# Gate and up bias of the experts: from TensorE products to rows loaded per job, spread by POOL and added by VectorE

## What is computed

```python
logits = jnp.dot(hf, w_router) + b_router
top_v, top_e = lax.top_k(logits, TOP_K)
top_w = jax.nn.softmax(top_v, axis=-1)
...
gu = xb @ w_gate_up[e] + b_gate_up[e]
gate = jnp.minimum(gu[:, 0::2], SWIGLU_LIMIT)
up = jnp.clip(gu[:, 1::2], -SWIGLU_LIMIT, SWIGLU_LIMIT)
act = (up + 1.0) * gate * jax.nn.sigmoid(SWIGLU_ALPHA * gate)
return act @ w_down[e] + b_down[e]
```

## Time and profile before

| | us |
|---|---|
| median of three runs | 1778.43 |
| lowest, highest | 1777.51, 1779.88 |
| profiled execution | 1780.92 |
| its span, first to last instruction | 1779.2 |
| mean granted TensorE clock, share of full | 0.977 |
| TensorE busy, share of the span | 1691.0, 95% |

### The profile page before, as it was taken

One profiled execution on the slowest core, in us unless ns is written; L12 is line 12 of the kernel. 1 busy time (PEld: TensorE's weight loads), 2 busy tenths in 40 slices (PEclk: granted clock), 3 DMA queues, 4 the chain that ended last, 5 costly groups with the idle time before them and its releaser, 6 DMA issues.

```text
span 1779.2 us, 43354 instructions
## 1 busy us (share of the span) xinstructions
PE 1691.0 (95%) x18644; PEld 885.3 (50%) x18644; DVE 577.8 (32%) x1366; ACT 350.2 (20%) x809; POOL 164.9 (9%) x250
## 2 busy tenths in 40 slices
PE   5999897689999888999999999999999999999997
PEld 2444896367478883434434434434434434434433
DVE  3679444664134564112112112112112112112211
ACT  3142321455222331101101101101101101101101
POOL 4000610101000001000000000000000000100100
PEclk9999999789999998999999999999999999999998
DMA  9950000401131259999999999999999999999991
GB/s 339 354 190 1 3 4 3 172 1 49 47 142 48 96 208 338 371 398 395 384 393 395 389 390 394 383 392 395 386 390 396 380 395 402 384 388 398 390 381 43
DMA packets 98345, 489.61 MB, mean 275 GB/s; under 512 B 15131, under 2 KB 17240, under 8 KB 48997
## 3 DMA queue, kind: packets, MB, share of 16 engines
q1 hardware_dynamic: 88326, 471.06, 67.4%
q0 software_dynamic: 7504, 16.80, 4.1%
q10 hardware_dynamic: 2448, 0.78, 0.2%
HBM read 478.87 MB, written 19.28 MB: 280 GB/s over the span
## 4 chain that ended last, share of the span: by engine, by line
PE 61%; DVE 0%; issue 0%; ACT 0%; POOLq 0%; DVEq 0%
PE bank L2090 37%; PE bank L2101 18%; PE bank L2075 1%; PE bank L2114 1%; PE bank L2081 1%; PE bank L2102 1%; PE bank L2091 1%; PE bank L2124 0%; DVE sb_y L2290 0%; POOLq L1979 0%; ACT sb_xT L2183 0%; DVE sb_mod L2281 0%; DVE sb_xT L2264 0%; ACT sb_wT L2206 0%; DVE sb_mod L2275 0%
## 5 line engine op out<-in xcount | busy, mean ns | idle before, releaser
L2090 PE MATMUL bank<-sb_w_raw,sb_xT 128*32 128x512 f32 x4608 | 668.7, 594 | 2.5 <-ACT sb_xT L2183 1.4
L2091 PE MATMUL bank<-sb_w_raw,sb_xT 128*32 128x512 f32 x1536 | 668.2, 594 | 0.0
L2090 PEld LDWEIGHTS bank<-sb_w_raw,sb_xT 128*32 128x32 f32 x4608 | 186.4, 110 | 455.9 <-issue 452.8
L2101 PE MATMUL bank<-sb_w_raw,sb_aT 128*32 128x256 f32 x4608 | 339.6, 381 | 2.0 <-DVE sb_aT L2271 2.0
L2102 PE MATMUL bank<-sb_w_raw,sb_aT 128*32 128x256 f32 x1536 | 339.2, 381 | 0.0
L2101 PEld LDWEIGHTS bank<-sb_w_raw,sb_aT 128*32 128x32 f32 x4608 | 188.5, 110 | 131.7 <-DVE sb_y L2290 2.3
L2275 DVE TENSOR_SCALAR sb_mod<-bank 128x256 f32<-128x256 f32 x96 | 40.5, 422 | 626.9 <-ACT sb_mod L2194 626.9
L2102 PEld LDWEIGHTS bank<-sb_w_raw,sb_aT 128*32 128x32 f32 x1536 | 166.9, 110 | 0.0
L2091 PEld LDWEIGHTS bank<-sb_w_raw,sb_xT 128*32 128x32 f32 x1536 | 166.3, 110 | 0.0
L2194 ACT ACTIVATE sb_mod<-bank 128x256 f32<-128x256 f32 x96 | 29.9, 384 | 655.6 <-PE bank L2091 655.6
L2290 DVE SCALAR_TENSOR_TENSOR sb_y<-bank,sb_prob_now,sb_mod 96x256 f32<-96x256 f32 x96 | 40.4, 474 | 215.1 <-PE bank L2102 215.1
(11 more groups left out here) (454 smaller groups left out, 1997.2 us busy)
## 6 DMA issues: line engine op xcount, KB each, us to landing
sb_w_raw<-in_w_gate_up_dram SPq DMA_DIRECT2D x256, 1024.0 KB, 8.1
sb_w_raw<-in_w_down_dram SPq DMA_DIRECT2D x128, 1024.0 KB, 8.5
sb_ring<-in_w_in_dram SPq DMA_DIRECT2D x7, 2048.0 KB, 10.0
sb_x<-in_ada_w_dram SPq DMA_DIRECT2D x8, 1024.0 KB, 9.0
sb_mod<-in_ada_w_dram SPq DMA_DIRECT2D x8, 1024.0 KB, 9.2
sb_ring<-in_ada_w_dram SPq DMA_DIRECT2D x3, 2048.0 KB, 14.0
sb_x<-in_x_dram SPq DMA_DIRECT2D x2, 2048.0 KB, 12.6
sb_ring<-in_w_out_dram SPq DMA_DIRECT2D x2, 2048.0 KB, 7.7
```

The costliest lines, as they stand in the source:

```text
L2090: te.matmul(up_bank[r][at, :], g.xT[:, k, at], g.w_raw[:, s, 512 * r:512 * r + 512], start=False, stop=last)
L2091: mm = te.matmul(up_bank[r][CAP:P, :], g.xT[:, k, STRIP * r:STRIP * r + STRIP], g.w_raw[:, s, 512 * G:2048], start=False, stop=last)
L2101: te.matmul(down_bank[j][at, 0:256], g.aT[:, k, at], g.w_raw[:, s, 1024 * r + 256 * j:1024 * r + 256 * j + 256], start=first, stop=last)
```

## The change

The bias rows are written once to DRAM with the one added to their odd entries. For every job ScalarE's queue loads the 8 KB row into one partition, POOL spreads it over all partitions (`partition_broadcast`, 1536 elements into `g.bias` and 512 into `g.last_quarter`), ScalarE copies the last quarter into partitions 96 to 127 of `g.bias`, and VectorE adds `g.bias` to the three banks into a new SBUF tile `g.biased`, from which gates and clips now read. The weights' products start the accumulation themselves. In the routing phase the bias takes two loads, two small ScalarE operations and two writes; the low parts are gone. At the start of the expert phase TensorE runs 20 filler products in place of the bias products.

```diff
+def load_bias(g, eng, e):
+    eng.dma_start(g.bias_row[0:1, :], g.bias_rows[e, :]).then_inc(g.row_in, 16)
...
 phase_route, sync
-            for i in range(2):
-                sp.dma_start(g.bias_raw[N_EXP * i:N_EXP * i + N_EXP, :, :], ...).then_inc(bias_in, 16)
-                at = slice(64 + N_EXP * i, 64 + N_EXP * i + N_EXP)
-                for j in range(G):
-                    sp.dma_start(g.bias_raw[at, j, :], g.a["b_gate_up"][0][:, 512 * G:]).then_inc(bias_in, 16)
+            sp.dma_start(wide_bias, g.a["b_gate_up"][0][:, 0:512 * G]).then_inc(bias_in, 16)
+            sp.dma_start(narrow_bias, g.a["b_gate_up"][0][:, 512 * G:]).then_inc(bias_in, 16)
...
+            sp.wait_ge(*act.at("bias_up"))
+            sp.dma_start(g.bias_rows[:, 0:512 * G], wide_bias).then_inc(g.bias_out, 16)
+            sp.dma_start(g.bias_rows[:, 512 * G:], narrow_bias).then_inc(g.bias_out, 16)
             for k in ks[4:]:
                 load_up(g, sp, k, slice(0, 1), k)
 phase_route, gpsimd: three memsets of g.pick go
 phase_route, scalar
-            sc.wait_ge(bias_in, 16 * (2 + 2 * G))
-            sc.copy(pairs(g.bias)[:, :, 0], pairs(g.bias_raw)[:, :, 0]).then_inc(*act("bias_even"))
-            sc.activation(pairs(g.bias)[:, :, 1], pairs(g.bias_raw)[:, :, 1], ACT.Identity, bias=g.ones[:, 0:1]).then_inc(*act("bias_hi"))
+            sc.wait_ge(bias_in, 16 * 2)
+            for part in (wide_bias, narrow_bias):
+                up = part.rearrange("p (n a) -> p n a", a=2)[:, :, 1]
+                mm = sc.activation(up, up, ACT.Identity, bias=g.ones[0:N_EXP, 0:1])
+            mm.then_inc(*act("bias_up"))
...
+            sc.wait_ge(g.bias_out, 16 * 2)
+            load_bias(g, sc, slice(0, 1))
 phase_route, vector
-            ve.wait_ge(*act.at("bias_hi"))
-            for i in range(2):
-                at = slice(64 * i + N_EXP, 64 * i + 2 * N_EXP)
-                raw, hi = pairs(g.bias_raw)[at], pairs(g.bias)[at]
-                ve.tensor_tensor(hi[:, :, 0], raw[:, :, 0], hi[:, :, 0].bitcast(F32), ALU.subtract)...
-                ve.scalar_tensor_tensor(hi[:, :, 1], raw[:, :, 1], 1.0, hi[:, :, 1].bitcast(F32), ALU.add, ALU.subtract)...
 phase_experts, sync
             e = expert(sp, last)
+            sp.wait_ge(g.row_in, 16 * last + 32)
 phase_experts, tensor
-            def bias_rows():
-                for b in range(G):
-                    mm = te.matmul(up_bank[b][:, :], g.bias_pick[:, :], g.bias[:, b, :], start=True, stop=False)
-                return mm
...
-                last = k == UP - 1
+                first, last = k == 0, k == UP - 1
...
-                        te.matmul(up_bank[r][at, :], ..., start=False, stop=last)
+                        te.matmul(up_bank[r][at, :], ..., start=first, stop=last)
...
-            te.wait_ge(*first_vec.at("bp0"))
-            bias_rows().then_inc(*first_pe("bias"))
+            for _ in range(20):
+                te.matmul(down_bank[2][:, 0:P], g.ones[:, :], g.ones[:, :], start=True, stop=True)
             te.wait_ge(x_in, 16)
...
                 activations_turned(turn, pe)
-                te.wait_ge(*vec.before("bp", turn))
-                bias_rows().then_inc(*pe("bias"))
 phase_experts, scalar
+            def quarter():
+                return sc.copy(g.bias[CAP:P, :, :], g.last_quarter[CAP:P, :].unsqueeze(1).broadcast_to([STRIP, G, 512]))
             def gated(b):
-                gate = up_bank[b][:, :].rearrange("p (n a) -> p n a", a=2)[:, :, 0]
+                gate = g.biased[:, b, :].rearrange("p (n a) -> p n a", a=2)[:, :, 0]
...
-            sc.wait_ge(used[UP - 1], 1)
+            sc.wait_ge(*pool.credit())
+            quarter().then_inc(*first_act("quarter"))
+            load_bias(g, sc, bass.ds(sc.value_load(g.table[0:1, 2:3], min_val=0, max_val=N_EXP - 1), 1))
             for b in range(G):
+                sc.wait_ge(*first_vec.at(f"ad{b}"))
                 gated(b).then_inc(*first_act(f"gc{b}"))
...
                 turned_copy().then_inc(*act("aT"))
-                sc.wait_ge(*done(UP_DONE, turn))
+                sc.wait_ge(*pool.at("spread", turn))
+                sc.wait_ge(*vec.before("ad2", turn))
+                quarter().then_inc(*act("quarter"))
+                load_bias(g, sc, bass.ds(expert(sc, turn + 2), 1))
                 sc.wait_ge(*vec.before("ac2", turn))
                 for b in range(G):
+                    sc.wait_ge(*vec.at(f"ad{b}", turn))
                     gated(b).then_inc(*act(f"gc{b}"))
 phase_experts, gpsimd
+            def spread():
+                po.partition_broadcast(g.bias[:, :, :].rearrange("p b n -> p (b n)"), g.bias_row[0:1, 0:512 * G])
+                return po.partition_broadcast(g.last_quarter[:, :], g.bias_row[0:1, 512 * G:])
             last = last_job(po)
+            po.wait_ge(g.row_in, 16)
+            spread().then_inc(*pool.credit())
...
             with po.Fori(0, last) as turn:
+                po.wait_ge(g.row_in, 16 * turn + 32)
+                po.wait_ge(*vec.before("ad2", turn))
+                po.wait_ge(*act.before("quarter", turn))
+                po.wait_ge(ticked, 3 * turn + 1)
+                tick(2)
+                spread().then_inc(*pool("spread"))
                 po.wait_ge(*vec.at("row", turn))
-                po.wait_ge(ticked, 2 * turn + 1)
+                po.wait_ge(ticked, 3 * turn + 2)
                 tick(0)
                 gather_rows(g, po, g.row[0:CAP, 0:1])
 phase_experts, vector (bias_pick and its uses go)
+            def added(b):
+                return ve.tensor_tensor(g.biased[:, b, :], up_bank[b][:, :], g.bias[:, b, :], ALU.add)
             def clipped(b):
-                ups = up_bank[b][:, :].rearrange("p (n a) -> p n a", a=2)[:, :, 1]
+                ups = g.biased[:, b, :].rearrange("p (n a) -> p n a", a=2)[:, :, 1]
...
+            ve.wait_ge(*first_act.at("quarter"))
+            ve.wait_ge(used[UP - 1], 1)
+            for b in range(G):
+                added(b).then_inc(*first_vec(f"ad{b}"))
...
                 turned_copy().then_inc(*vec("aT"))
-                ve.wait_ge(*pe.at("bias", turn))
-                bias_pick(bass.ds(turn + 2, 1)).then_inc(*vec("bp"))
+                ve.wait_ge(*act.at("quarter", turn))
+                ve.wait_ge(*done(UP_DONE, turn))
+                for b in range(G):
+                    added(b).then_inc(*vec(f"ad{b}"))
```

More of the change, by code:

```diff
@@ L1691, in phase_route @@
         merge = rows[:, 128:160]
+        wide_bias = g.bias[0:N_EXP, :, :].rearrange("p s n -> p (s n)")
+        narrow_bias = g.bias[N_EXP:2 * N_EXP, 0, :]
         mask, block_sum, mask_one = g.mask, g.block_sum, rows[:, 256:384].rearrange("p (t e) -> p t e", t=NT)
@@ L1987, in phase_experts @@
         up_bank, down_bank, turn_bank = ps[0:3], ps[3:6], ps[6:8]
-        pe = Turns(g.sem(ctx, "m_pe"), ["tr0", "tr1", "bias", "xt0", "xt1"])
-        act = Turns(g.sem(ctx, "m_act"), ["aT", "gc0", "gc1", "gc2", "xh", "y"])
-        vec = Turns(g.sem(ctx, "m_vec"), ["aT", "bp", "uc0", "ac0", "uc1", "ac1", "uc2", "ac2", "row", "xl", "share", "goal", "yw", "y"])
+        pe = Turns(g.sem(ctx, "m_pe"), ["tr0", "tr1", "xt0", "xt1"])
+        act = Turns(g.sem(ctx, "m_act"), ["aT", "quarter", "gc0", "gc1", "gc2", "xh", "y"])
+        vec = Turns(g.sem(ctx, "m_vec"), ["aT", "ad0", "ad1", "ad2", "uc0", "ac0", "uc1", "ac1", "uc2", "ac2", "row", "xl", "share", "goal", "yw", "y"])
+        pool = Turns(g.sem(ctx, "m_pool"), ["spread"])
         used = [g.sem(ctx, f"used{i}") for i in range(SLOTS)]
@@ L1997, in phase_experts @@
         x_in, y_out = g.x_in, g.sem(ctx, "y_out")
-        first_pe = g.steps(ctx, "first_pe", ["bias", "xt0", "xt1", "wT"] + names("bd{}", 3) + ["xt2"])
-        first_act = g.steps(ctx, "first_act", ["xh", "wT", "gc0", "gc1", "gc2"])
-        first_vec = g.steps(ctx, "first_vec", ["bp0", "y", "xl", "bp1"] + [x for i in range(2 * NT) for x in (f"gb{i}", f"xb{i}")] + [x for b in range(G) for x in (f"uc{b}", f"ac{b}")])
+        first_pe = g.steps(ctx, "first_pe", ["xt0", "xt1", "wT"] + names("bd{}", 3) + ["xt2"])
+        first_act = g.steps(ctx, "first_act", ["xh", "wT", "quarter", "gc0", "gc1", "gc2"])
+        first_vec = g.steps(ctx, "first_vec", ["y", "xl"] + [x for i in range(2 * NT) for x in (f"gb{i}", f"xb{i}")] + names("ad{}", G) + [x for b in range(G) for x in (f"uc{b}", f"ac{b}")])
         last_pe = g.steps(ctx, "last_pe", ["tr0", "tr1", "d"])
@@ L2008, in phase_experts, with expert @@
         UP_DONE, DOWN_DONE = SPARE - 1, UP - 1
+        def expert(eng, job):
+            return eng.value_load(g.table[0:1, bass.ds(job + 1, 1)], min_val=0, max_val=N_EXP - 1)
         def last_job(eng):
@@ L2036, in _ @@
         def _(sp):
-            def expert(job):
-                return sp.value_load(g.table[0:1, bass.ds(job + 1, 1)], min_val=0, max_val=N_EXP - 1)
             def rest_of_turn(turn, e, after):
@@ L2056, in _ @@
             with sp.Fori(1, last) as turn:
```

(12 more changed lines are left out.)

35 lines of the change are left out of this document (12 added, 23 removed).

## The result

The changed kernel takes 1760.76 us (median of four runs, 1758.08 to 1767.13) against 1779.16 us for the kernel before on the same chip: a ratio of 0.9911, 95% interval 0.9891 to 0.993. The forecast was 1762.2 us. The profiled execution took 1759.59 us (span 1757.8) against 1780.92.

What follows compares the result with a forecast made beforehand. TensorE was taken to set the 33.55 us turn, DMA close behind with some 22 us of loads in hand. Terms -21.7 + 2.2 + 1.6 + 1.7 = -16.2 us gave 1762.2 us; range 1753 to 1771, 8 in 10.

Steps and rivals of the forecast that it cites:

- The matmuls out of the loop, -21.7 us: Head of each loop turn: three bias matmuls leave TensorE's path, 0.70 us in each of 31 turns, at most -26.0.
- Additions under cover: VectorE in the loop: three additions, 2.06 us ahead of the clips, cost nothing since 6 us remain before TensorE's transposes.
- Spread on POOL "1.9 us, nothing": POOL's two broadcasts in each turn: 1.9 us taken from a memset's rate, 20.8 at the dear end, covered either way.
- 22 in hand: Cover for POOL's spread in a loop turn: TensorE waits at its transposes only once the spread takes over 22 us.
- Rival (b): TensorE's transposes in the loop: POOL's spread outlasts its cover, 9.3 us wait a turn, 2050 us total; chance 0.05.
- The row's own DMAs: nothing: Bias row load in each turn: 8 KB on ScalarE's queue against 12 MB on SP's costs nothing.
- DMA at the shorter turn: nothing, at most 1 us: Weight loads at 32.85 us turns: even needing 33.55 us they bind only at the very end, under 1 us.
- Rival (a): Loop: DMA becomes the bound, needing say 34.0 us a turn, total 1776.6 us; chance 0.07.
- the rule I set aside: DMA in the loop: HBM reads limited to about 358 GB/s a core, 37 us a turn; rejected for measured 395 GB/s.
- First job +2.2: Start of expert stage: 20 fillers replace bias matmuls, first six groups end at 687.4 against 685.1; bounds -1.2 to +6.2.
- its end +1.6: First job's end: VectorE's additions stand uncovered on the path, 2.06 us less a 0.41 us wait for ScalarE.
- Clock fall ahead of the loop, +1.7: After the first job: TensorE idles 2.6 us, then a low-clock stretch costs 1.7 us; bounds 0 and +3.4.

Runs made afterwards that it cites:

- experiment 1: Kernel before the change, with its gate/up bias products and VectorE's selector left out of the loop, nothing in their place: 1752.98 us, ratio 0.9856.
- experiment 2: Changed kernel with three products of the old bias shape put back at the head of each loop turn, result overwritten: 1780.4 us, ratio 1.0027.
- experiment 4: Changed kernel with one more one-column elementwise operation between POOL's two broadcasts of a turn: 2272.43 us, one run.
- experiment 5: Changed kernel with POOL's ticks given as semaphore increments on its queue in place of one-column products: 1759.89 us, ratio 0.9908.
- experiment 7: Changed kernel without the 20 filler products at the start of the expert phase: 1756.24 us, ratio 0.9891.
- experiment 6: Changed kernel with 20 filler products ahead of the loop in place of 12: 1761.48 us, ratio 0.9927.
- experiment 9: Changed kernel with each bias row stored and loaded in 16 pieces of 512 B, 1024 B apart in DRAM: 1761.79 us, ratio 0.9923.

## Why the prediction was right, and which of its terms were not

**The matmuls out of the loop, -21.7 us: right.** Turns of 32.85 us, the first group still 0.56. Experiments 1 and 2 show it from both sides. So is the reading behind it, that TensorE and not DMA set the turn in the kernel before, as experiment 1 got all 31 x 0.70 us.

**Additions under cover: right.** 1.89 us for three, against 2.06; TensorE waits for none of them in a normal turn.

```profile
1260.93 1.89 DVE L2288 TENSOR_TENSOR sb_biased<-bank,sb_bias 128x512 f32<-128x512 f32 x3 [19.19 <-PE bank L2086]
```

**Spread on POOL "1.9 us, nothing": right in the sum, wrong in its working.** The two operations are 2.6 us; the memset was a fair neighbour. But I priced the data that move and not the change from one kind of operation to another, 8.3 us there and 9 back; no row of the kernel before showed such a change. With the spread and the later scatter it took 13.6 us of the 22 in hand, and in turn 0, where POOL first waits for the output to be written, it came through: turn 1 is +1.0 us. The order of waits that the prediction takes for a normal turn does not hold in the first. Rival (b) named the right place; experiment 4 is what it looks like.
The Trainium skill (GPSIMD Engine Reference, Instruction dispatch) gives about 6 us for the first call of freshly loaded code on this engine. It is the rule I should have weighed. This case agrees with its kind and not with its size or its number: 8.3 to 10.8 us, and at every change of operation, not once. That it is code being loaded is inferred from the `MODIFY_POOL_CONFIG` records, which come with the idle time (after, experiment 4) and go with it (experiment 5).

**"The row's own DMAs: nothing": wrong.** It was argued from 8 KB against 12 MB. By the needs (33.28 without the row, 33.51 to 33.60 with it in four kernels, 33.26 and 33.35 in 16 pieces) one row of two 4 KB packets costs 0.2 to 0.3 us a turn; by the 34.7 with four rows, 0.4 for each further one.

**"DMA at the shorter turn: nothing, at most 1 us": right in place, small in size.** I took 33.55 us a turn as the worst that the row allowed and put the bound at the very end. The true need is 33.56, because the row's load had made up what the old kernel had spare (33.28); the loads were late in turns 28 and 29 and cost 0.43 + 1.04 = 1.5 us. Rival (a) would have needed 34.0.
As for the rule I set aside there, the Trainium skill (Perfetto Trace Analysis, Roofline, the note on utilization above 100%) limits the 358 GB/s to two active cores of a pair, and puts a single one's ceiling at some 435. This kernel runs on one core, and the 395 GB/s of the normal turn above agree with the note.

**First job +2.2 and its end +1.6: 2 us too dear together, +1.7 measured** (76.34 against 74.60 from routing's first product to the loop). The fillers' clock rose some 3 us after their start and not 7.0, so they took 6.22 us and not 8.0; the first product came 8.25 us after their start, not 10.3. The low clock around the stage's start was one piece in the kernel before (667.6 to 684.7) and is two short ones now (663.8 to 667.2 and 670.6 to 674.0); the prediction had no row that told where they would fall. What I did not ask was whether they were worth anything: by experiment 7 they were the dearest part of the change outside the loop, 3.65 us in that pair and 2 to 4 over all kernels.

**Clock fall ahead of the loop, +1.7: right, by luck in part.** Idle 2.08 us (forecast 2.6), low for 3.4 us, turn 0 +1.63. But with the same gap two other kernels showed no fall.

So the sum -16.2 against -15.8 holds two errors that cancel: about 2 us too dear ahead of the loop, and 2.5 us too cheap in it (1.5 late loads, 1.0 late spread). That the medians came within 1.4 us of the forecast is luck in part as well: the runs of one kernel spread over 7 to 9 us, and stretches without any changed instruction differ by 5.6.

## What to carry to other kernels

When one engine is relieved, measure the next resource by the growth of its landing times (turn length plus growth a turn) and not by its busy share: here DMA showed 1.01 at 33.28, 33.56 and 34.7 us of need alike, as long as no load was late. Compare such needs at the same turn length. Count a small transfer by what it does to the queue it joins, not by its bytes; where DMA is near the bound, two large packets for one partition cost as much as some 120 KB spread out (0.3 us at 395 GB/s). And before an engine gets a new kind of operation, look at what it does before and after it: a one-column elementwise operation cost more than the broadcast it stood beside.

## What was not expected of the hardware

- POOL, going from an elementwise operation to a partition broadcast or back, stood idle 8.3 to 10.8 us each time (the change, experiments 4 and 6), with `MODIFY_POOL_CONFIG` records on its sequencer. Indirect DMAs beside a broadcast brought none of it (experiment 5). The broadcasts themselves took 1.80 us for 1536 and 0.80 us for 512 elements a partition.
- An 8 KB load of two packets cost the weight loads around it 0.2 to 0.4 us a turn, and about nothing as 32 packets. Whether it is one DMA engine or the way into one partition that the large packets hold up stays open: the trace has no engine for a packet. The bytes, the queue and the partition were the same; what experiment 9 changed is the size and number of the packets and, with them, the spacing in DRAM, and these are not told apart.
- A gap of 2.1 us on TensorE ahead of the loop was followed by half clock in six kernels and by none in two; gaps of 0.3 and 1.0 us by none in four.
